# Expert weights of a mixture-of-experts loop loaded from two queues, SyncE's and GpSimd's, in place of one

## The chip, the cores and the metric

The kernel runs on one core of one Trainium2 chip, in float32 throughout. The metric is device time in microseconds (us). A profiled execution also has a span, from its first to its last instruction.

## The reference

One step of a two-layer trunk over 128 context tokens and 128 latent tokens of width 1024. Each layer is an attention block followed by a mixture of 16 experts, of which each token takes two. The experts' part, cut to what matters:

```
def _moe(h, w_router, b_router, w_gate, w_up, w_down):
    ...                                     # gates: two experts of one group for each token
    hid = jax.nn.silu(jnp.einsum('nd,edf->enf', n, w_gate)) * jnp.einsum('nd,edf->enf', n, w_up)
    hid = hid * gates.T[:, :, None].astype(hid.dtype)
    return jnp.einsum('enf,efd->nd', hid, w_down).reshape(b, s, d)
```

`w_gate`, `w_up` and `w_down` are 1024x1024 for each of 16 experts and each of two layers: 96 matrices of 4.2 MB, 403 MB together, each read once from HBM. The outputs are both token groups after two layers and the new keys and values.

## The kernel before

The program is written by hand, engine by engine, with semaphores; the order on each engine is the order in the code, and no scheduler stands between. Each engine's block (`@block.sync`, `@block.gpsimd`, `@block.tensor`) is one instruction stream.

**Pairs and units.** The experts of a layer are worked through in eight pairs, n = 0 to 7. A pair has two experts, e = 0 (the first) and e = 1 (the second), and each matrix is cut into two halves, so that a pair has `MOE_UNITS` = 12 units of 2 MB: k = 0 to 3 are the halves of `w_gate`, 4 to 7 those of `w_up`, 8 to 11 those of `w_down`. Even k belong to e = 0, odd k to e = 1. A unit is written (n, k) below. One load of a unit moves 128 rows of 16 KB, one row to a partition.

**Products.** TensorE works through a pair in six products (`product(n, k, ...)`, L1190), for k = 0, 2, 4, 6, 8, 10. Product (n, k) needs units (n, k) and (n, k+1) together: its 32 matmuls go alternately to the two experts, which occupy the two halves of the array. Between the products stand the scatter of the pair before (L1151, behind product 0) and the transposes and the gather of the next pair (L1246 and L1140, behind product 6).

**The ring.** The units lie in `SLOTS` = 6 buffers of 2 MB (`ring`, with the list `MOE_RING` giving the order). Six is even, so that in the loop three of the slots only ever take first experts' units and three only second experts'. With the last matmul that reads a slot, TensorE raises `moe_used[l]` by one. The load of (n, k) waits until that count is at least `n * MOE_UNITS + (k + 1)`, that is until the unit six places earlier has been used. In pairs 0 to 2 some units go to other buffers (`ahead`, and the tiles named by `kept_rows`): these use none of the ring's turns.

**The loads.** All loads of units are issued by SyncE, in the order of use: pairs 0 to 2 written out (`load_early`, L577), pairs 3 to 6 in a hardware loop over `units_of`, with `load_in_turn` for each unit (wait at L582), and pair 7 by `last_units`: k = 0 to 5 as whole units, and from k = 6 on in pieces of half or a quarter of a unit (`LAST_PIECES`, L640), so that TensorE can begin on a part (`last_product`, L1216). A second round of pairs, in which the counts of tokens would call for it, doesn't take place with these inputs. Behind the experts of layer 0 SyncE goes on to the dense weights of layer 1.

GpSimd computes a few powers (L774), and issues small loads and stores through its own queue. The last thing that it does ahead of a layer's experts is the power for the router's norm.

Of the kernel before, what the change touches and what calls it, by code (L numbers as in the profile page):

```python
# [256 lines left out]
def build(nc, a):  # L257
    ctx = ExitStack()
    with ctx:
# [3 lines left out]
        def sem(name):  # L263
            return ctx.enter_context(nc.semaphore(name))
# [124 lines left out]
        dense_ld = [sem(f"dense_loaded{i}") for i in range(SLOTS)]  # L389
        moe_used = [sem(f"moe_used{l}") for l in range(LAYERS)]  # L390
        moe_ld = [[sem(f"moe_loaded{l}_{i}") for i in range(SLOTS)] for l in range(LAYERS)]
        last_ld = [[sem(f"last_loaded{l}_{i}") for i in range(len(LAST_PIECES))] for l in range(LAYERS)]
        ahead_ld = [[sem(f"ahead_loaded{l}_{e}") for e in range(2)] for l in range(LAYERS)]
        ld_first, ld_const, ld_vec, ld_gb, ld_small, ld_router = (
            sem(n) for n in ("ld_first_const", "ld_const", "ld_vec", "ld_gate_bias", "ld_small", "ld_router"))
# [1 line left out]
        ld_cache = [sem(f"ld_cache{l}") for l in range(LAYERS)]  # L397
        ld_bias = sem("ld_bias")
        turns = sem("turns")
        gbuf_unit_loaded = sem("gbuf_unit_loaded")  # L400
        out_kv = [sem(f"out_kv{l}") for l in range(LAYERS)]
        out_y = sem("out_y")
# [78 lines left out]
        def moe_slot(l, k):  # L481
            return MOE_RING[l][k % SLOTS]
# [76 lines left out]
        def _(sp):  # L559
# [9 lines left out]
            def experts(l):  # L569
# [50 lines left out]

                def units_of(n, i):

                    at = [sp.snap(i * (2 * D * D) + e * D * D) for e in range(2)]
                    for k in range(MOE_UNITS):
                        load_in_turn(k, at[k % 2], n * MOE_UNITS + (k + 1))

                def last_units(n):

                    at = [(2 * (PAIRS - 1) + e) * D * D for e in range(2)]
                    for k in range(LAST_PIECES[0][0]):  # L630
                        load_in_turn(k, at[k % 2], n * MOE_UNITS + (k + 1))
                    for i, (k, c0, c1) in enumerate(LAST_PIECES):
                        w, order = (a["w_up"], "(p h r) -> h p r") if k < 8 else (a["w_down"], "(h p r) -> h p r")
                        for e in range(2):
                            slot = moe_slot(l, k + e - OUTSIDE)
                            src = w[l].rearrange("e k n -> (e k n)")[at[e]:at[e] + D * D].rearrange(order, h=2, p=P)[k // 2 % 2]
                            if c0 == 0:
                                sp.wait_ge(moe_used[l], n * MOE_UNITS + (k + e + 1))
                            cols = slice(D * c0, D * c1)
                            sp.dma_start(flat[slot][:, cols], src[:, cols]).then_inc(last_ld[l][i], 16)  # L640

                def load_first(k):
                    slot = moe_slot(l, k)
# [122 lines left out]
        def _(pool):  # L766
# [33 lines left out]
            def spread_gates(l):  # L800
# [8 lines left out]
                for t in (1, 0):  # L809
                    pool.dma_start(gbuf[:, 2 * t:2 * t + 2, :].rearrange("p u n -> p (u n)"),  # L810
                                   gate_rows[l, t].partition_broadcast(P)).then_inc(gate_spread[t], 16)

            for l in range(LAYERS):
                if l == 1:
                    power("norm", 1, 0, 1)
                    power("norm", 1, 0, 0)
                    pool.wait_ge(filled, fill(("qkv", 1, 0, 1)))
                    rpb = a["c_rpb"]
                    for d in range(3):
                        src = bass.AP(rpb.tensor, rpb.offset + (d + 6) * 31, [[15 * 31, 16], [0, 64], [1, 32]])  # L820
                        pool.dma_start(copies[:, d, :, :], src).then_inc(bias_copied, 16)
                    pool.wait_ge(filled, fill(("qkv", 1, 1, 1)))
                    pool.dma_start(cache[:, 0:1024], a["cache_c_k"][0, 0].rearrange("k h d -> k (h d)")).then_inc(ld_cache[1], 16)
                    pool.dma_start(cache[:, 1024:2048], a["cache_c_v"][0, 0].rearrange("k h d -> k (h d)")).then_inc(ld_cache[1], 16)
                    pool.wait_ge(bias_copied, 48)
                    for r in range(2):
                        for r2 in range(2):
                            src = bass.AP(copies.tensor, copies.offset + (r2 - r + 1) * 64 * 32 + 15, [[31, 64], [3 * 64 * 32, 16], [1, 64]])
                            pool.dma_start(bias[64 * r:64 * r + 64, :, 64 * r2:64 * r2 + 64], src).then_inc(ld_bias, 16)
                power("qk", l, 1)  # L830
                power("qk", l, 0)

                pool.wait_ge(normed, 2 * l + 2)
                pool.wait_ge(*emptied_by(("qkv", l, IN_UNITS[l] - 1, 0)))
                if l == 0:
                    outs = [("new_a_k", 512, 128), ("new_a_v", 640, 128), ("new_b_k", 1280, 512), ("new_b_v", 1792, 512)]
                else:
                    outs = [("new_c_k", 1024, 1024), ("new_c_v", 2048, 1024)]
                for name, at, n in outs:
                    pool.dma_start(a[name], qkv[0][:, at:at + n]).then_inc(out_kv[l], 16)  # L840
                if l == 0:
                    power("sub", 0, 1)
                spread_gates(l)
                if l == 0:
                    power("sub", 0, 0)
                power("norm", l, 1, 1)
                power("norm", l, 1, 0)
            pool.wait_ge(out_kv[0], 64)
            pool.wait_ge(out_kv[1], 32)

# [2 lines left out]
        def _(pe):  # L853
# [272 lines left out]
            def experts(l):  # L1126
# [27 lines left out]
                def product(n, k, banks, lhs, ready, half_done=None):  # L1154
# [6 lines left out]
                    for e in range(2):  # L1161
                        if apart[e]:
                            pe.wait_ge(m["kept_loaded1" if n else f"kept_loaded{e}"], 16 * (KEPT_LOADS[1, l] + KEPT_AGAIN if n else KEPT_LOADS[e, l]))
                        elif slots[e] is None:
                            pe.wait_ge(ahead_ld[l][e], 16 * (n + 1) + (16 if (n, k) == (2, SLOTS + 2) else 0))
                        else:
                            pe.wait_ge(moe_ld[l][slots[e]], (0 if early else 32 * n) + 16 * (1 + turn_of[e] // SLOTS))

                    def weights(e, c, j):
                        if l == 1 and early and (n, k, c) == (0, 0, 3):  # L1170
# [34 lines left out]
                def last_product(n, k, banks, lhs, half_done):  # L1205
# [3 lines left out]
                    for i, (unit, c0, c1) in enumerate(LAST_PIECES):  # L1209
                        if unit != k:  # L1210
                            continue
                        pe.wait_ge(last_ld[l][i], 32)
                        for j in range(2):
                            for c in range(c0, c1):
                                for e in range(2):
                                    ins = pe.matmul(bank[banks[j]][64 * e:64 * e + 64, :], lhs[:, 4 * h + c, 64 * e:64 * e + 64],  # L1216
                                                    rows4[slots[e]][:, c, j * UC:(j + 1) * UC],
                                                    start=(h, c) == (0, 0), stop=(h, c) == (1, 3), tile_position=(0, 64 * e))
                                    if (j, c) == (1, 3):
                                        ins.then_inc(moe_used[l], 1)  # L1220
                            if half_done and (c1, j) == (4, 0):
                                ins.then_inc(half_done, 1)
# [916 lines left out]
```

## Time and profile before

| | |
|---|---|
| time, median of 3 runs | 1244.72 us (1243.37 to 1246.33) |
| the profiled execution: time, span | 1242.9 us, 1241.1 us |
| TensorE busy | 1164.1 us, 94% |
| VectorE, ScalarE, GpSimd busy | 279.8, 187.7, 56.4 us |
| moved by DMA | 494.18 MB, mean 398 GB/s |
| of it from SyncE's queue, from GpSimd's | 485.88 MB, 7.46 MB |
| mean TensorE clock granted | 0.988 of full speed |

All of these but the first row are of one execution under the profiler. Its queue q1 is SyncE's, `hardware_dynamic`; q0 is GpSimd's, `software_dynamic`. A queue's share is the time that its packets took, as a share of the time of the core's 16 DMA engines. "Us to landing" runs from the issue of a DMA to the rise of its semaphore. A matmul group that waited shows in square brackets the idle time ahead of it and what ended it. `PEld` is the load of weights into the array, which runs beside the matmuls.

### The profile page before, as it was taken

The page shows a single profiled execution, that of the slowest core. Times are in us where ns is not written, and L with a number is a line of the kernel's source. Part 1 is how long each engine was busy: PE and PEld are TensorE (multiplying, and loading weights), DVE is VectorE, ACT ScalarE, POOL GpSimd, SP SyncE. Part 2 cuts the span into 40 slices and gives each one's busy share as a digit, 9 for nine tenths or more (in the row PEclk, how much of TensorE's full clock was granted, in tenths as well). Part 3 has the DMA queues.
Part 4 walks back from the last instruction along what each step waited for, and adds up shares of the span by engine and source line. Part 5 has one row for each costly group of instructions (what it writes and reads, how often), then busy time and mean ns, then how long its engine had stood idle before and what let it go on. Part 6 is the DMA issues. An engine that isn't in the chain of part 4 may idle for free.

```text
span 1241.1 us, 13752 instructions
## 1 busy us (share of the span) xinstructions
PE 1164.1 (94%) x5533; PEld 515.1 (42%) x5533; DVE 279.8 (23%) x673; ACT 187.7 (15%) x441; POOL 56.4 (5%) x68
## 2 busy tenths in 40 slices
PE   4999999999988899899999999999999998989898
PEld 1445464443423233334344454753434434343333
DVE  1146533121010101021232354312021110202013
ACT  1224322010000000001021343210001100000010
POOL 0412000000000000000013020000000000000000
PEclk9999999999999999999999999999999999999999
DMA  9999999999999999999997559899999999999997
GB/s 375 383 383 375 414 423 429 424 431 427 429 427 427 429 429 428 429 427 429 420 392 259 203 196 397 339 391 413 426 428 428 428 428 428 428 430 428 427 425 296
DMA packets 60084, 494.18 MB, mean 398 GB/s; under 512 B 5490, under 2 KB 6658, under 8 KB 28420
## 3 DMA queue, kind: packets, MB, share of 16 engines
q1 hardware_dynamic: 56992, 485.88, 94.5%
q0 software_dynamic: 2864, 7.46, 1.9%
q8 instruction: 33, 0.54, 0.2%
q10 hardware_dynamic: 180, 0.17, 0.0%
q14 instruction: 15, 0.12, 0.0%
HBM read 490.72 MB, written 3.16 MB: 398 GB/s over the span
## 4 chain that ended last, share of the span: by engine, by line
PE 72%; DMA 24%; issue 2%; ACT 1%; SPq 1%; DVE 1%; POOL 0%; DVEq 0%
PE bank L1190 39%; PE bank L942 12%; DMA ring<-in_w_up 9%; DMA ring<-in_w_gate 7%; DMA ring<-in_w_down 6%; PE bank L952 3%; PE bank L1140 3%; PE bank L898 3%; PE bank L1151 3%; DMA ring<-in_w_in_ab 2%; PE bank L874 2%; PE bank L1216 1%; PE bank L959 1%; PE bank L997 1%; PE bank L1246 1%
## 5 line engine op out<-in xcount | busy, mean ns | idle before, releaser
L1190 PE MATMUL bank<-ring,hT 128*64 128x512 f32 x2520 | 574.3, 606 | 48.0 <-issue 20.1
L1190 PEld LDWEIGHTS bank<-ring,hT 128*64 128x64 f32 x2520 | 191.2, 139 | 401.6 <-issue 392.8
L942 PE MATMUL bank<-ring,hT 128*128 128x512 f32 x320 | 141.8, 600 | 3.1 <-DMA ring<-in_w_in_ab 2.4
L942 PEld LDWEIGHTS bank<-ring,hT 128*128 128x128 f32 x320 | 60.5, 192 | 79.9 <-issue 77.3
L1983 DVE TENSOR_TENSOR work<-work,bank 128x512 f32<-128x512 f32 x56 | 38.5, 688 | 164.0 <-PE bank L1151 163.8
L1976 DVE TENSOR_TENSOR work<-work,bank 128x512 f32<-128x512 f32 x32 | 22.0, 688 | 223.6 <-PE bank L1190 198.8
L1190 PE MATMUL bank<-work,hT 128*64 128x512 f32 x284 | 69.5, 593 | 0.0
L1140 PE MATMUL bank<-work 128*128 128x128 f32 x512 | 60.3, 275 | 0.0
L1140 PEld LDWEIGHTS bank<-work 128*128 128x128 f32 x512 | 58.7, 192 | 1.6 <-issue 1.6
L1519 ACT ACTIVATE hT<-bank 128x512 f32<-128x512 f32 x32 | 19.0, 595 | 256.9 <-PE bank L1246 256.9
L2024 DVE COPY work<-bank 128x512 f32<-128x512 f32 x14 | 9.7, 692 | 207.3 <-PE bank L1190 207.3
L1151 PE MATMUL bank<-work 128*128 128x512 f32 x112 | 51.8, 605 | 0.0
L898 PE MATMUL bank<-ring,cond 128*32 128x512 f32 x384 | 47.4, 616 | 2.4 <-DMA ring<-in_w_mod 2.0
L1216 PE MATMUL bank<-ring,hT 128*64 128x512 f32 x192 | 42.9, 595 | 4.0 <-DMA ring<-in_w_down 4.0
L1964 DVE TENSOR_TENSOR work<-work,bank 128x512 f32<-128x512 f32 x32 | 22.0, 688 | 106.9 <-ACT work L1528 106.9
L952 PE MATMUL bank<-ring,work 128*128 128x512 f32 x96 | 42.5, 595 | 0.3 <-DVE work L1793 0.3
L1190 PEld LDWEIGHTS bank<-work,hT 128*64 128x64 f32 x284 | 22.8, 137 | 41.8 <-issue 41.4
L1546 ACT ACTIVATE work<-bank 128x512 f32<-128x512 f32 x14 | 8.4, 597 | 191.2 <-PE bank L1190 191.2
L1528 ACT ACTIVATE work<-bank 128x512 f32<-128x512 f32 x32 | 19.1, 597 | 108.5 <-PE bank L1190 108.5
L1151 PEld LDWEIGHTS bank<-work 128*128 128x128 f32 x112 | 20.1, 189 | 31.5 <-issue 31.5
L1454 ACT ACTIVATE work<-bank,nm 128x256 f32<-128x256 f32 (+1 forms) x64 | 26.0, 421 | 29.7 <-DVE nm L1766 29.7
L774 POOL TENSOR_TENSOR ss<-ss,const 128x1 f32<-128x1 f32 x8 | 4.4, 556 | 553.1 <-DVE ss L1640 498.6
(220 smaller groups left out, 754.4 us busy)
## 6 DMA issues: line engine op xcount, KB each, us to landing
ring<-in_w_gate SPq DMA_DIRECT2D x56, 2048.0 KB, 17.7
ring<-in_w_up SPq DMA_DIRECT2D x50, 2048.0 KB, 17.2
ring<-in_w_down SPq DMA_DIRECT2D x46, 2048.0 KB, 17.0
ring<-in_w_mod SPq DMA_DIRECT2D x23, 2048.0 KB, 11.1
work<-in_w_up SPq DMA_DIRECT2D x8, 2048.0 KB, 15.2
ring<-in_w_down SPq DMA_DIRECT2D x14, 1024.0 KB, 14.7
ring<-in_w_in_c SPq DMA_DIRECT2D x6, 2048.0 KB, 21.1
ring<-in_w_in_ab SPq DMA_DIRECT2D x4, 2048.0 KB, 21.6
```

The costliest lines, as they stand in the source:

```text
L874: ins = pe.transpose(b[:, i * P:(i + 1) * P], src, K("ident"))
L898: ins = pe.matmul(out, cond[:, 2 * k + r, :], cols, start=(k, r) == (0, 0), stop=(k, r) == (3, 1), tile_position=(0, 32 * j))
L942: ins = pe.matmul(b[:, 0:n], hT[:, c, t * P:(t + 1) * P], w[:, c, 0:n], start=i == 0, stop=i == DC - 1)
L952: ins = pe.matmul(b[:, :], oT(l, t, c), w[:, c, :], start=c == 0, stop=c == DC - 1)
L1140: ins = pe.matmul(to[:, c * P:(c + 1) * P], htok(t)[:, at:at + P], pick[:, t, :], start=t == 0, stop=t == 1)
L1151: pe.matmul(bank[4 + 2 * t + h][:, :], GT[:, t, :], yd[:, h * UC:(h + 1) * UC], start=True, stop=True).then_inc(m["scattered"], 1)
L1190: ins = pe.matmul(bank[banks[j]][64 * e:64 * e + 64, :], lhs[:, 4 * h + c, 64 * e:64 * e + 64], weights(e, c, j), start=(h, c) == (0, 0), ...
L1216: ins = pe.matmul(bank[banks[j]][64 * e:64 * e + 64, :], lhs[:, 4 * h + c, 64 * e:64 * e + 64], rows4[slots[e]][:, c, j * UC:(j + 1) * UC] ...
L1454: ins = act.activation(PR[:, j % 2, h, 0:nk], bank_of(("S", l, t, b, e))[:, i * nk:(i + 1) * nk], ACT.Exp, bias=nm[:, j % 2, h:h + 1], sca ...
L1964: dve.tensor_tensor(hid[:, half], sg[:, half], bank[h][:, :], ALU.mult).then_inc(m["gate_taken"], 1)
L1976: dve.tensor_tensor(hid[:, half], hid[:, half], bank[2 + h][:, :], ALU.mult).then_inc(m["hid_done"], 1)
L1983: dve.tensor_tensor(y[:, t, cols], y[:, t, cols], bank[4 + 2 * t + h][:, :], ALU.add).then_inc(m["y_added"], 1)
```

## The change

For pairs 3 to 7 of each layer the loads of the second expert's whole units (odd k: six a pair in pairs 3 to 6, and k = 1, 3, 5 of pair 7) are issued by GpSimd, each after its own wait on `moe_used[l]` with the number it had on SyncE. SyncE keeps the even ones, with their waits, and both experts' pieces from k = 6 of pair 7 on. GpSimd's loads raise semaphores of their own (`pool_ld`, three a layer), and TensorE waits for these in place of the ring's (`moe_ld`) where e = 1. The semaphores of the last pieces are shared by the two layers. Sizes, sources, destinations, slots and the order within each expert are as they were.

```diff
+        pool_ld = [[sem(f"pool_loaded{l}_{i}") for i in range(SLOTS // 2)] for l in range(LAYERS)]
...
                 def units_of(n, i):
 
-                    at = [sp.snap(i * (2 * D * D) + e * D * D) for e in range(2)]
-                    for k in range(MOE_UNITS):
-                        load_in_turn(k, at[k % 2], n * MOE_UNITS + (k + 1))
+                    at = sp.snap(i * (2 * D * D))
+                    for k in range(0, MOE_UNITS, 2):
+                        load_in_turn(k, at, n * MOE_UNITS + (k + 1))
...
-                    for k in range(LAST_PIECES[0][0]):
-                        load_in_turn(k, at[k % 2], n * MOE_UNITS + (k + 1))
+                    for k in range(0, LAST_PIECES[0][0], 2):
+                        load_in_turn(k, at[0], n * MOE_UNITS + (k + 1))
...
+            def experts(l):
...
+                def load_in_turn(k, at, wait):
+                    w, half = matrix_of(k)
+                    slot = moe_slot(l, k - OUTSIDE)
+                    pool.wait_ge(moe_used[l], wait)
+                    pool.sem_inc(turns, 1)
+                    flat_w = w[l].rearrange("e k n -> (e k n)")[bass.ds(at, D * D)]
+                    order = "(h p r) -> h p r" if k >= 8 else "(p h r) -> h p r"
+                    pool.dma_start(flat[slot], flat_w.rearrange(order, h=2, p=P)[half]).then_inc(pool_ld[l][k % SLOTS // 2], 16)
+
+                def units_of(n, i):
+
+                    at = pool.snap(i * (2 * D * D) + D * D)
+                    for k in range(1, MOE_UNITS, 2):
+                        load_in_turn(k, at, n * MOE_UNITS + (k + 1))
...
+                    for k in range(1, LAST_PIECES[0][0], 2):
+                        load_in_turn(k, at, n * MOE_UNITS + (k + 1))
+
+                with pool.Fori(3, PAIRS - 1) as i:
+                    units_of(i, i)
...
+                last_units(more * PAIRS + (PAIRS - 1))
...
                 power("norm", l, 1, 1)
                 power("norm", l, 1, 0)
+                experts(l)
...
-                        else:
+                        elif early or not e:
                             pe.wait_ge(moe_ld[l][slots[e]], (0 if early else 32 * n) + 16 * (1 + turn_of[e] // SLOTS))
+                        else:
+                            pe.wait_ge(pool_ld[l][(k + 1) % SLOTS // 2], 32 * n + (16 * (1 + turn_of[e] // SLOTS) - (80 if (k + 1) % SLOTS == 5 else 64)))
...
-                        pe.wait_ge(last_ld[l][i], 32)
+                        pe.wait_ge(last_ld[i], 32 * (l + 1))
```

SyncE, the body of the loop over pairs 3 to 6 in layer 0, before; the numbers behind `ring` are the slots, the two experts' units alternate, and the register instruction between two loads sets the next wait.

```order
L577 DMA ring4<-in_w_gate 128x4096
L581 REGISTER_ALU
L577 ISA
L577 DMA ring5<-in_w_gate 128x4096
L581 REGISTER_ALU
L577 ISA
L577 DMA ring3<-in_w_gate 128x4096
L581 REGISTER_ALU
L577 ISA
L577 DMA ring1<-in_w_gate 128x4096
L581 REGISTER_ALU
L577 DMA ring2<-in_w_up 128x4096
```

And in the changed kernel, the same body from its first load to its last:

```order
L578 DMA ring4<-in_w_gate 128x4096
L582 REGISTER_ALU
L578 ISA
L578 DMA ring3<-in_w_gate 128x4096
L582 REGISTER_ALU
L578 DMA ring2<-in_w_up 128x4096
L582 REGISTER_ALU
L578 DMA ring4<-in_w_up 128x4096
L582 REGISTER_ALU
L578 DMA ring3<-in_w_down 128x4096
L582 REGISTER_ALU
L578 ISA
```

The loads to slots 5, 1 and 0 have left SyncE's stream, which now holds six loads a pair, to slots 4, 3 and 2.

GpSimd, from the last power ahead of the experts of layer 0, in the changed kernel (before, the next instruction behind this power was layer 1's first):

```order
L775 TENSOR_TENSOR ss<-ss,const 128x1 x2
L840 UNCONDITIONAL_BRANCH
L840 ISA
L826 ISA
L826 DMA ring5<-in_w_gate 128x4096
L822 REGISTER_ALU
L826 ISA
L826 DMA ring1<-in_w_gate 128x4096
L822 REGISTER_ALU
L826 DMA ring0<-in_w_up 128x4096
L822 REGISTER_ALU
L826 DMA ring5<-in_w_up 128x4096
```

The first of these loads is unit (3, 1). It stands behind no load of pairs 0 to 2, all of which SyncE still issues.

## Rows read from the trace of the kernel before

**Rows 1.** The page: DMA engines, busy tenths and GB/s in 40 slices of 31 us.

```profile
...
DMA  9999999999999999999997559899999999999997
GB/s 375 383 383 375 414 423 429 424 431 427 429 427 427 429 429 428 429 427 429 420 392 259 203 196 397 339 391 413 426 428 428 428 428 428 428 430 428 427 425 296
...
```

**Rows 2.** Busy time by stretch: columns in the first row, DMA share and GB/s last.

```profile
...
core 0: us, PE busy (x) PEld busy (x) DVE busy (x) ACT busy (x) POOL busy (x), PEclk, DMA share, GB/s
...
253.00:303.00 50.00, 50.00 (x244) 19.84 (x242) 7.74 (x17) 4.46 (x8) 0.00 (x0) 1.00 1.01 428
...
400.00:450.00 50.00, 43.72 (x206) 17.84 (x202) 7.04 (x16) 4.45 (x8) 0.00 (x0) 0.97 1.01 428
...
```

**Rows 3.** TensorE, 328 to 354 us.

```profile
...
328.71 7.09 PE L1190 MATMUL bank<-work,hT 128*64 128x512 f32 x32
336.04 7.09 PE L1190 MATMUL bank<-ring,hT 128*64 128x512 f32 x32 [0.24 <-issue]
345.97 7.09 PE L1190 MATMUL bank<-ring,hT 128*64 128x512 f32 x32 [2.84 <-DMA ring<-in_w_gate]
...
```

**Rows 4.** L577, issues between 320 and 326 us, time to landing.

```profile
...
L577 SPq DMA_DIRECT2D ring<-in_w_gate x2: 332/332/333, 324.3 to 324.9; - x2
...
DMA to landing us min/median/max: 26.3/28.5/30.6
```

**Rows 5.** DMA queues, 400 to 450 us.

```profile
...
DMA packets 1472, 21.41 MB, mean 428 GB/s; under 512 B 165, under 2 KB 165, under 8 KB 165
...
q1 hardware_dynamic: 1472, 21.41, 100.6%
...
```

**Rows 6.** GpSimd behind the experts of layer 0.

```profile
...
636.20 0.55 POOL L774 TENSOR_TENSOR ss<-ss,const 128x1 f32<-128x1 f32 x1 [454.13 <-DVE ss L1640]
...
655.17 0.55 POOL L824 DMA_DIRECT2D work<-in_cache_c_v  x1
...
```

**Rows 7.** TensorE, 600 to 633 us, the tail of layer 0.

```profile
...
600.56 7.09 PE L1190 MATMUL bank<-ring,hT 128*64 128x512 f32 x32 [0.50 <-DMA ring<-in_w_up]
...
614.44 1.61 PE L1246 MATMUL bank<-const,work 128*128 128x128 f32 x8
...
625.31 7.09 PE L1216 MATMUL bank<-ring,hT 128*64 128x512 f32 x32 [1.42 <-DMA ring<-in_w_down]
632.39 1.98 PE L1237 MATMUL bank<-work 128*128 128x512 f32 x4
...
```

**Rows 8.** SyncE's queue, 299 to 344 us.

```profile
...
317.43 7.85 SPq L577 DMA_DIRECT2D ring<-in_w_gate  x4
343.24 10.85 SPq L577 DMA_DIRECT2D ring<-in_w_up  x4
...
```

**Rows 9.** Every DMA issue of the kernel: a small store, us to landing.

```profile
...
out_y_sample<-x SPq DMA_DIRECT2D x2, 256.0 KB, 2.1
...
```

**Rows 10.** DMA queues, 134 to 137 us.

```profile
...
q1 hardware_dynamic: 107, 0.87, 68.5%
q0 software_dynamic: 104, 0.42, 34.2%
...
```

**Rows 11.** DMA queues, 758 to 761 us.

```profile
...
q0 software_dynamic: 236, 0.85, 70.3%
q1 hardware_dynamic: 24, 0.38, 29.3%
...
```

**Rows 12.** DMA queues, 156 to 165 us.

```profile
...
DMA packets 367, 3.83 MB, mean 426 GB/s; under 512 B 35, under 2 KB 35, under 8 KB 163
...
q1 hardware_dynamic: 366, 3.82, 100.7%
...
```

**Rows 13.** DMA queues, 656 to 660 us.

```profile
...
q0 software_dynamic: 96, 0.39, 25.1%
...
```

**Rows 14.** DMA queues, 745 to 753 us.

```profile
...
DMA packets 684, 3.49 MB, mean 436 GB/s; under 512 B 135, under 2 KB 135, under 8 KB 540
...
```

**Rows 15.** DMA queues, 130.6 to 140 us.

```profile
...
DMA packets 1005, 3.90 MB, mean 415 GB/s; under 512 B 32, under 2 KB 32, under 8 KB 768
...
```

## What the change was predicted to do

> **What bounds the kernel now.** I began with the page's slices. The DMA engines stand at 9 tenths from the start to some 640 us and again from some 800 us to the end, at 424 to 431 GB/s wherever experts are loaded at full rate; only around layer 1's attention do they fall, to 5 [rows 1]. The busy times by stretch show what this means for TensorE: between 253 and 303 us it is busy for the whole 50 us, between 400 and 450 us for 43.72, while the engines show a share of 1.01 and 428 GB/s in both [rows 2]. So TensorE is the faster of the two: a pair is 12 loads of 2.097 MB, which take 58.8 us at 428 GB/s, 4.9 us each. In the first pairs it lives on units loaded ahead; from layer 0's pair 2 on it waits, as for the gate units of product (3, 0) at 345.97 us [rows 3]. SyncE's own time doesn't enter: the loads that it issued at 324.3 and 324.9 us landed only after 26.3 and 30.6 us [rows 4]. The end of the experts is set by bytes over rate.
>
> The queue list gives the form of the load. From 400 to 450 us there were 1472 packets, 165 of them under 512 B; the other 1307 carry 21.41 MB, 16 KB each: one row of a unit. They cost 1.006 x 50 / 21.41 = 2.35 us of all engines per MB [rows 5].
>
> **What moves.** GpSimd takes 24 loads a layer in pairs 3 to 6 and 3 in pair 7: 54 loads, 113 MB. While both queues feed the engines SyncE moves as much; 226 MB at 428 GB/s is a stretch of 529 us. Here a change of rate counts: 1% is 5.3 us.
>
> **Issue.** One costs SyncE 0.33 us [rows 4]. For GpSimd the nearest row is a cache's load, 0.55 us [rows 6]; it needs six in 58.8 us and has nothing else to do for 454 us ahead of the power at 636.20 us [rows 6]. What hides the issue is the backlog of two loads or more, 9.8 us. On GpSimd only its own next loads stand behind a waiting one, and behind layer 0's that power, over 30 us after product (7, 4) began at 600.56 us [rows 7]. Without the cover 27 issues a layer cost 0.22 us more each, 12 us in all. I take 0.
>
> **Which load goes first.** SyncE issued (3, 0) at 317.43 us and the next three up to 325.3 us [rows 8]. Before, (3, 1) and (3, 3) stood behind everything older. Now they are in a queue of their own and take part at once. Before, (3, 3) landed at 324.9 + 30.6 = 355.5 us [rows 4]; stepping back by 4.9 us a load, (2, 11) landed at about 335.9 us, and TensorE began product (2, 10) at 336.04 [rows 3]. GpSimd's two loads can overtake by 9.8 us at most, since (3, 5) has to wait for a slot. So (2, 11) lands at 345.7 us, product (2, 10) ends at 352.8, and only then are (3, 4) and (3, 5) issued, (3, 4) at 343.24 before [rows 8]. Do the engines run dry? What was issued by 324.9 us lasts until 355.5 us as before, 2.7 us longer. A load's start costs less: a store of 256 KB, 0.6 us of transfer, landed after 2.1 us [rows 9]. Product (3, 0) starts some 7 us late but finds (3, 1) to (3, 3) landed or nearly so, and the lag is made up in a few products, each of which takes TensorE 7.1 us and the engines 9.8. Cost 0. If the margin failed, each us beyond it would cost a us a layer.
>
> **Tail.** With half for each queue, both units of a product land when the second of them landed before. From 600.56 us TensorE has four products of 7.1 us and transposes of 1.61 us, up to 630.5 us, where its last product ended at 632.39 [rows 7]. So (7, 5) may land 1.9 us late for nothing. Where GpSimd gets more than half, the last bytes are SyncE's, and nothing is lost either. The sharing itself is seen twice: from 134 to 137 us 104 packets of GpSimd's (4 KB) ran beside 107 of SyncE's (8 KB) [rows 10]; from 758 to 761 us GpSimd's 4 KB packets moved 0.85 MB beside 0.38 MB of SyncE's 16 KB packets [rows 11]. GpSimd's queue wasn't held back in either. I take half and half, and 0.
>
> The Trainium skill ("DMA: Bandwidth & Descriptors", section "Queues, rings and completion order") says that each engine takes turns between queues packet by packet. The first stretch agrees, 104 to 107; the second doesn't, since by that rule GpSimd's small packets would have had a fifth of the bytes. By the rule the sum would be the same here as long as both sides use 16 KB packets.
>
> **A GpSimd packet's price.** No row shows one of 16 KB. SyncE's 4 KB packets: from 156 to 165 us there were 128 (163 less the 35 small ones), 0.52 MB; of 9.06 us in all the other 3.30 MB take 7.75, which leaves 2.52 us per MB [rows 12]. GpSimd's, loading a cache: 0.251 x 4 / 0.39 = 2.57 us per MB [rows 13]. The 0.05 is 0.003 us a packet on one engine. Taken per packet, 8 packets an engine a load and 54 loads give 432 x 0.0033 = 1.4 us; taken per byte, 5.7 us. I take 1.4, since the size changes and the count of events is what a packet's overhead goes with. Below, a gain isn't excluded: see the third rival.
>
> **Sum.** The profiled execution took 1242.9 us (span 1241.1), and 1.4 makes 1244.3. The median of the runs is 1.8 above that execution, so 1246.1 us: no change that could be told, for I count 0.2% (2.5 us) as what a measurement here can tell.
>
> **The rivals.**
>
> *SyncE's queue is favoured* (slower). If it gets clearly more than half, the pieces of (7, 6) and (7, 7), 9.8 us of transfer, go ahead of (7, 5), and the tail starts that much late: 9.8 - 1.9 = 7.9 us a layer, 15.8 in both, 1262 us. It decides from 1.9 us of lag. The two stretches of rows 10 and 11 speak against it. 0.13.
>
> *GpSimd's rows are cut into 4 KB packets* (slower): 2.57 in place of 2.35 us per MB on 113 MB is 25 us, 1271 us, and by turns of packets the first rival comes on top. For it speaks only that every large GpSimd packet in the trace is of 4 KB, and so are the rows there. 0.10. The Trainium skill ("DMA: Bandwidth & Descriptors", section "SWDGE vs HWDGE vs iDMA") prefers packets of at most 4096 B where GpSimd builds them; no run here shows such a cut, since every row was short enough.
>
> *Two queues fill the engines better* (faster). A packet of one queue can hide the other's gap. From 745 to 753 us, with both at work, 436 GB/s were moved [rows 14], 1.9% above 428: 9.9 us over the stretch, 1235 us at best; a third to a half of it, some 1241, is likelier, because GpSimd's part there was stores. 0.22.
>
> *A few engines are slowed by GpSimd's queue* (slower). A load is complete with its slowest engine, and all of them are full, so the mean rate falls. With GpSimd's packets in the mix 415 GB/s were moved from 130.6 to 140 us [rows 15]; against 428 that is 3%, 16 us over 529, but SyncE's rows of 8 KB and less explain part of it, so 5 to 16 us, 1251 to 1262. 0.09. The Trainium skill ("DMA: Bandwidth & Descriptors", section "Latency and other measured facts") puts a like slowness of two engines down to the rings that GpSimd writes, as a guess; this profile shows no single engine.
>
> **How the numbers follow.** The forecast has 0.46, its own range being 1243 to 1248. Faster is 0.22; slower is 0.13 + 0.10 + 0.09 and 0.02 of the forecast's upper end, 0.34; the same 0.44. The range runs from 1239, which leaves out the better part of the third rival's gain, 0.08, to 1263, which leaves out the cut rows, 0.10.
>
> **What will show it.** Right: SyncE and GpSimd each some 50% of the engines between 400 and 450 us, 1307 large packets there, and 428 GB/s; product (2, 10) about 10 us late, product (3, 6) on its old time; the last products of both layers as before. Wrong: more packets than 1472 in that window (cut rows); a rate other than 427 to 429; idle engines near 355 us; or (7, 5) landing after 602.5 us while SyncE's pieces are in.

## The result, and the profile after

The changed kernel took 1246.64 us (median of 20 runs, 1244.24 to 6849.65), the kernel before beside it 1243.77 us (20 runs, 1242.37 to 1246.76). The ratio is 1.0025, 95% interval 1.0015 to 1.0036: some 3 us slower, a little past the 0.2% that had been set as the limit of what can be told. The forecast was 1246.1 us and "no change". One of the 20 runs took 6849.65 us; the next longest took 1259.0. It is left out of the ratio, no later run of any kernel repeated it, and it stays unexplained. The profiled execution took 1245.49 us, span 1243.8, that is 2.6 and 2.7 more than before.

**The page**, whose slices answer to [rows 1], differs in one place worth a look:

```profile
...
GB/s 374 391 375 375 414 423 429 423 432 428 427 382 428 429 429 428 427 429 428 422 394 281 204 186 398 337 384 419 423 429 424 427 429 428 429 428 427 429 423 300
...
```

Slice 12 (342 to 373 us, counting from 1) has 382 GB/s in place of 427. The other slices of layer 0's pairs have 422 to 432, before 420 to 431. This is the part in which the second queue takes up its work in layer 0.

**In the steady part** of layer 0 the queues look as predicted (compare [rows 2, 5]):

```profile
...
DMA packets 1469, 21.45 MB, mean 429 GB/s; under 512 B 160, under 2 KB 160, under 8 KB 160
...
q0 software_dynamic: 735, 10.73, 50.5%
q1 hardware_dynamic: 734, 10.72, 50.3%
...
```

735 packets for 10.73 MB beside 734 for 10.72: half and half, and GpSimd's rows go as one packet of 16 KB each, not cut. Their price is 0.505 x 50 / 10.73 = 2.353 us of all engines per MB, SyncE's 2.346. On 113 MB that makes 0.8 us by this row; the prediction had 1.4.

**Busy times by stretch** (last columns: granted clock, DMA share, GB/s):

```profile
...
core 0: us, PE busy (x) PEld busy (x) DVE busy (x) ACT busy (x) POOL busy (x), PEclk, DMA share, GB/s
335.00:345.00 10.00, 1.00 (x6) 0.11 (x2) 0.00 (x0) 0.00 (x0) 0.00 (x0) 0.67 1.00 424
345.00:355.00 10.00, 9.04 (x36) 3.25 (x38) 0.69 (x1) 0.54 (x1) 0.00 (x0) 0.81 0.78 331
355.00:365.00 10.00, 10.00 (x40) 3.72 (x36) 2.12 (x4) 0.06 (x1) 1.06 (x2) 1.00 0.98 390
400.00:450.00 50.00, 43.01 (x198) 17.07 (x194) 7.73 (x17) 3.37 (x6) 2.64 (x5) 0.97 1.01 429
1060.00:1110.00 50.00, 44.46 (x208) 18.65 (x205) 7.73 (x17) 4.14 (x8) 2.64 (x5) 0.97 1.01 428
...
```

429 and 428 GB/s in the steady parts of the two layers, as before. But from 345 to 355 us the engines moved 331 GB/s at a share of 0.78, and then 390; before it was 426 and 428. This is (428 - 331) x 10 + (428 - 390) x 10 us, 1.35 MB, or 3.2 us of all engines. A closer look at the hole:

```profile
...
345.00:348.00 3.00, 2.04 (x6) 0.85 (x8) 0.00 (x0) 0.00 (x0) 0.00 (x0) 0.50 1.03 437
351.00:352.00 1.00, 1.00 (x6) 0.31 (x4) 0.69 (x1) 0.00 (x0) 0.00 (x0) 1.00 0.81 344
352.00:353.00 1.00, 1.00 (x8) 0.37 (x6) 0.00 (x0) 0.00 (x0) 0.00 (x0) 1.00 0.65 279
353.00:354.00 1.00, 1.00 (x8) 0.40 (x6) 0.00 (x0) 0.00 (x0) 0.00 (x0) 1.00 0.12 49
354.00:354.50 0.50, 0.50 (x4) 0.15 (x2) 0.00 (x0) 0.04 (x1) 0.00 (x0) 1.00 0.00 0
354.50:355.00 0.50, 0.50 (x4) 0.15 (x2) 0.00 (x0) 0.50 (x1) 0.00 (x0) 1.00 0.08 33
355.00:355.50 0.50, 0.50 (x4) 0.15 (x2) 0.00 (x0) 0.06 (x1) 0.41 (x1) 1.00 0.13 33
355.50:356.00 0.50, 0.50 (x6) 0.21 (x4) 0.00 (x0) 0.00 (x0) 0.12 (x1) 1.00 2.26 492
357.00:358.00 1.00, 1.00 (x6) 0.31 (x4) 0.00 (x0) 0.00 (x0) 0.00 (x0) 1.00 0.84 360
...
```

The rate fell from 351 us on, to 49 GB/s between 353 and 354. From 354.0 to 355.0 us a single packet started, the 16 KB that make the 33 GB/s of the last half microsecond, and the flow came back at 355.5. A window counts a packet where it starts, so the shares of such short windows are rough; the old rate stands again from 358 on. By the bytes missing from 352 to 358 us the hole is 3.2 us of all engines.

The 16 engines did not run out together. A load raises its semaphore sixteen times, in the trace's single records, and a product waits for the last of these; each load's raises have the same spacing as those of the load before it, shifted by 4.9 us, as if each belonged to one engine. For (3, 2), the last load queued, fifteen came between 352.2 and 354.2 us and the last at 355.63, mean 353.4. The last packet ended at 355.15 us, 0.5 before the last raise. So one engine was some 1.5 us behind the others and worked almost until the flow came back, while the average engine was done at about 352.9 us (the mean raise less that 0.5, an estimate). Before, the raises of (3, 3) lie alike: fifteen from 352.1 to 353.9 us, the last at 355.5. The spread is not the second queue's work.

**Why they ran empty** is read from the views below. First SyncE's queue (start, length, issues in the group):

```profile
...
317.63 7.20 SPq L578 DMA_DIRECT2D ring<-in_w_gate  x2
354.53 7.20 SPq L578 DMA_DIRECT2D ring<-in_w_up  x2
...
```

And GpSimd's issues, each with the wait ahead of it:

```profile
...
318.20 0.59 POOL L826 DMA_DIRECT2D ring<-in_w_gate  x1 [135.94 <-PE bank L1232]
325.40 0.54 POOL L826 DMA_DIRECT2D ring<-in_w_gate  x1 [6.61 <-issue]
355.10 0.53 POOL L826 DMA_DIRECT2D ring<-in_w_up  x1 [29.16 <-PE bank L1232]
...
```

GpSimd issued (3, 1) at 318.20 us and (3, 3) at 325.40, each with 0.53 to 0.59 us (0.55 predicted). They landed 15.4 and 18.0 us later, at 333.6 and 343.4, while the same trace has SyncE's (3, 0) and (3, 2), issued at 317.6 and 324.5, landing after 33.1 and 31.1 us. In between both queues moved bytes at once (320 to 328 us):

```profile
...
q1 hardware_dynamic: 130, 1.88, 55.3%
q0 software_dynamic: 92, 1.51, 44.6%
...
```

So the older loads in SyncE's queue had to give way. The landing of the two units (2, 10) and (2, 11):

```profile
...
L578 SPq DMA_DIRECT2D ring<-in_w_down x2: 327/379/431, 310.5 to 310.9; - x2
...
DMA to landing us min/median/max: 28.0/31.5/35.0
```

310.9 + 35.0 = 345.9 us, where the prediction had 345.7 and before it was about 335.9. TensorE (compare [rows 3]):

```profile
...
328.91 7.09 PE L1232 MATMUL bank<-work,hT 128*64 128x512 f32 x32
345.96 15.31 PE L1232 MATMUL bank<-ring,hT 128*64 128x512 f32 x64 [9.96 <-issue]
...
365.05 20.94 PE L1232 MATMUL bank<-ring,hT 128*64 128x512 f32 x96
...
408.34 7.09 PE L1232 MATMUL bank<-ring,hT 128*64 128x512 f32 x32 [2.73 <-DMA ring<-in_w_gate]
...
```

After product (2, 8) TensorE stood for 9.96 us, and products (2, 10) and (3, 0) together took 15.31 us in place of two times 7.09 less the overlap, 13.95. The first window of the fine view shows why: from 345 to 348 us the granted clock was 0.50, the lower of TensorE's two levels, 1.2 GHz. It cost this pair 1.4 us. The Trainium skill ("TensorE: Matmul & The Clock Gate", section "What's actually happening") has the clock fall when the engine is idle; the row agrees. Only at 354.53 us did SyncE issue (3, 4), at 355.10 GpSimd (3, 5). The last load queued until then, (3, 2), landed at 324.5 + 31.1 = 355.6 us. The lag stays: product (3, 6), the third in the row at 365.05 us, began at 379.0 (375.19 before), product (4, 0) at 408.34 (404.69 before), and the layer's last product (compare [rows 7]) ended 2.7 us late:

```profile
...
589.89 20.88 PE L1232 MATMUL bank<-ring,hT 128*64 128x512 f32 x96
610.58 7.07 PE L1258 MATMUL bank<-ring,hT 128*64 128x512 f32 x32
...
627.97 7.09 PE L1258 MATMUL bank<-ring,hT 128*64 128x512 f32 x32 [1.39 <-DMA ring<-in_w_down]
635.06 1.98 PE L1279 MATMUL bank<-work 128*128 128x512 f32 x4
...
```

The row at 589.89 holds the three products up to (7, 4), 96 matmuls without a wait. The waits of the pieces behind it are 0.16 and 1.39 us, before 0.60 and 1.42.

**Accounting by layer**, from the profiles. For layer 0 I take the instant at which TensorE's small group behind the last scatter begins: 634.21 us before, 636.88 after, +2.67. For layer 1 I take the time from its first expert product to its last scatter: 433.95 before, 434.02 after. So in this pair of executions all of the 2.7 us came in layer 0, where the bytes went missing between 345 and 365 us, and the 0.8 us of the packets doesn't show.

### The profile page after: what moved, and what is told of

Same layout as the page of the kernel before. It is cut to its first block, busy times and chain, and to the rows that moved or that the text cites. A ratio compares the mean times of both kernels' runs of the same rounds, so it can differ in the third digit from the quotient of the medians.

```text
span 1243.8 us, 13780 instructions
## 1 busy us (share of the span) xinstructions
PE 1163.7 (94%) x5533; PEld 514.6 (41%) x5533; DVE 279.6 (22%) x673; ACT 187.6 (15%) x441; POOL 85.0 (7%) x122
## 4 chain that ended last, share of the span: by engine, by line
PE 65%; DMA 31%; issue 2%; ACT 1%; DVE 1%; SPq 0%; POOLq 0%; POOL 0%; DVEq 0%
PE bank L1232 34%; DMA ring<-in_w_gate 13%; PE bank L982 12%; DMA ring<-in_w_up 11%; DMA ring<-in_w_down 5%; PE bank L992 3%; PE bank L938 3%; PE bank L1180 2%; DMA ring<-in_w_in_ab 2%; PE bank L1191 2%; PE bank L914 2%; PE bank L1258 1%; PE bank L999 1%; PE bank L1037 1%; PE bank L1271 1%
## 5 line engine op out<-in xcount | busy, mean ns | idle before, releaser
L826 POOL DMA_DIRECT2D ring<-in_w_gate x20 | 10.7, 534 | 445.0 <-PE bank L1232 426.8
L775 POOL TENSOR_TENSOR hss<-hss,const 128x28 f32<-128x28 f32 (+2 forms) x6 | 22.6, 3764 | 116.2 <-DVE hss L1641 116.2
```

Of the source, the lines that this page charges most:

```text
L775: pool.tensor_tensor(v, v, K("mhalf")[:, 0:v.shape[1]], ALU.pow).then_inc(power_taken, 1)
```

## The experiments

The expectations speak of two theories. **A**: the loss is the overtaking at the place where the second queue begins. **B**: it is a cost of the second queue itself, spread over its 54 loads. Ratios are against the kernel before, run on the same chip, with 95% intervals; "layer 0" is the shift of the instant defined above, in one profiled execution. Kernels 1 and 5 have the same program for layer 0 and stand at 0.0 and +1.7, so a difference of that size between two rows can be chance.

| kernel | median us | ratio | layer 0 |
|---|---|---|---|
| the change | 1246.64 | 1.0025 [1.0015, 1.0036] | +2.7 |
| 1: first two on SyncE, layer 0 | 1244.96 | 1.0018 [1.0003, 1.0034] | 0.0 |
| 2: before, only the first two on GpSimd | 1246.78 | 1.0025 [1.0016, 1.0034] | +2.5 |
| 3: before, the first four on GpSimd | 1251.32 | 1.0059 [1.0047, 1.0072] | +12.1 |
| 10: before, only the first on GpSimd | 1243.03 | 0.9998 [0.9989, 1.0006] | -0.1 |
| 5: first two on SyncE, both layers | 1243.62 | 1.0004 [0.9993, 1.0015] | +1.7 |
| 4: 34 idle matmuls behind (2, 8) | 1246.44 | 1.0023 [1.0011, 1.0034] | +5.5 |
| 6: 16 and 16 idle matmuls | 1246.01 | 1.0021 [1.0011, 1.0030] | +3.2 |
| 9: 16 and 26 idle matmuls | 1246.78 | 1.0033 [1.0019, 1.0047] | +1.5 |
| 7: GpSimd's rows in 4 KB pieces | 1263.45 | 1.0157 [1.0139, 1.0175] | +15.2 |
| 8: SyncE's rows in 4 KB pieces | 1262.34 | 1.0150 [1.0132, 1.0169] | +12.4 |

### 1. Without the overtaking in layer 0

```diff
+                if l == 0:
+                    for k in (0, 1, 2, 3, 4, 6, 8, 10):
+                        slot = moe_slot(l, k - OUTSIDE)
+                        sp.wait_ge(moe_used[l], 3 * MOE_UNITS + (k + 1))
+                        load(k, (6 + k % 2) * D * D, flat[slot], first_ld[k // 2] if k % 2 else moe_ld[l][slot])
-                with sp.Fori(3, PAIRS - 1) as i:
+                with sp.Fori(4 if l == 0 else 3, PAIRS - 1) as i:
...
```

SyncE keeps (3, 1) and (3, 3) of layer 0, and GpSimd begins there with (3, 5).

> The changed kernel, except that in layer 0 units (3, 1) and (3, 3) stay in SyncE's queue; GpSimd begins with (3, 5), so nothing overtakes pair 2's loads. Two loads of 256 B into a scratch row take the place of the two on GpSimd's semaphores. Theory A (the loss is one pause of the DMA engines near 355 us, made by the two loads that overtake): the span falls back by 2.7 us to about 1241.1, ratio to the kernel before 1.000, product (2, 10) of layer 0 begins near 336.0 us again, and 428 GB/s are moved from 345 to 400 us. Theory B (each GpSimd packet costs more than SyncE's, over all 54 loads): 52 of the 54 loads are still GpSimd's, so the ratio stays at 1.0025.

Layer 0 behaved as A says. Two stretches, the one in which the engines were short in the changed kernel, and one of layer 1:

```profile
...
345.00:355.00 10.00, 8.99 (x33) 2.99 (x34) 0.00 (x0) 0.00 (x0) 0.00 (x0) 0.83 1.01 428
...
950.00:955.00 5.00, 5.00 (x26) 1.89 (x24) 0.17 (x1) 0.60 (x1) 0.53 (x1) 1.00 1.00 390
...
```

428 GB/s from 345 to 355 us, and the layer is back at its old end. The ratio isn't 1: 1.0018, its interval just free of 1. In this execution layer 1 took 435.88 us, 1.9 more than before, with 390 GB/s from 950 to 955 us, which makes 0.4 us of it; the rest isn't placed. The kernel still overtakes in layer 1, where I had expected nothing.

### 2, 3 and 10. The overtaking alone, with two loads, four and one

Based on the kernel before; `first_ld` holds k = 1 and 3, then 0 to 3, then 1 alone. All else stays with SyncE. Pair 3's loads are written out for this, and the semaphores of the last pieces are shared as in the change; kernel 10 has the same edits, so it also shows what they cost: nothing.

```diff
+                if l == 0:
+                    for k in first_ld:
+                        pool.wait_ge(moe_used[l], 3 * MOE_UNITS + (k + 1))
+                        src = a["w_gate"][l].rearrange("e k n -> (e k n)")[(6 + k % 2) * D * D:(7 + k % 2) * D * D]
+                        pool.dma_start(flat[moe_slot(l, k - OUTSIDE)], src.rearrange("(p h r) -> h p r", h=2, p=P)[k // 2]).then_inc(first_ld[k], 16)
...
```

> The complement: the kernel before, except that units (3, 1) and (3, 3) of layer 0 are GpSimd's, and nothing else. Theory A: the whole loss with 2 of the 54 loads, ratio 1.0025, product (2, 10) near 346 us, the engines paused near 355 us. Theory B: 2/54 of the loss, 0.1 us, ratio 1.000.

> As the run with the first two, but all four gate units of pair 3 of layer 0, (3, 0) to (3, 3), are GpSimd's: the overtaking doubled. Theory A: at half and half the four take 19.6 us of transfer and SyncE's backlog at 318 us is 17.8 us, so (2, 11) lands near 353.6 us, product (2, 10) ends near 362.4 at the slow clock, and the engines stand still from about 355.5 us (last byte 2 us earlier) until some 364: 8 to 11 us are lost, ratio 1.0065 to 1.009. Theory B: 4/54 of the loss, ratio 1.000.

> The kernel before, except that unit (3, 1) of layer 0 alone is GpSimd's: the overtaking halved against the run with two. Theory A: 4.9 us are overtaken, (2, 11) lands near 340.8 us, product (2, 10) ends near 348 to 349.5, 6 us before what is queued runs out, so the engines never stop and nothing is lost: ratio 1.000. A loss in proportion to the overtaking would give half of that with two loads, 1.0012.

Two loads on GpSimd, with 52 fewer than in the change, lose all that the change loses. TensorE in kernel 2:

```profile
...
345.62 15.42 PE L1203 MATMUL bank<-ring,hT 128*64 128x512 f32 x64 [9.44 <-issue]
...
```

And SyncE's queue there:

```profile
...
354.24 7.67 SPq L578 DMA_DIRECT2D ring<-in_w_up  x4
...
```

The same wait, the same slow pair of products, the same late issue. B is refuted as the cause of this loss. With four loads product (2, 10) came at 353.49 us (worked out ahead as 353.6) and the next issue on SyncE at 363.54; the engines stood for nearly a whole stretch. TensorE in kernel 3:

```profile
...
353.49 16.83 PE L1203 MATMUL bank<-ring,hT 128*64 128x512 f32 x64 [10.05 <-issue]
...
```

And the busy times by stretch:

```profile
...
355.00:365.00 10.00, 10.00 (x39) 3.33 (x37) 0.69 (x1) 0.60 (x1) 0.00 (x0) 0.78 0.12 28
...
```

The loss was 7.3 us by the ratio and 8.0 by the medians, in the profiled execution 12, which is the longest of the six: the expectation of 8 to 11 was a little high for the median. With one load product (2, 10) came at 340.94 us (340.8 worked out), the issue at 350.71, and nothing was lost. TensorE in kernel 10:

```profile
...
340.94 16.56 PE L1203 MATMUL bank<-ring,hT 128*64 128x512 f32 x64 [4.53 <-issue]
...
```

And SyncE's queue:

```profile
...
350.71 7.67 SPq L578 DMA_DIRECT2D ring<-in_w_up  x4
...
```

One, two and four loads that overtake delay product (2, 10) by 4.9, 9.6 and 17.5 us, yet they cost 0, about 3 and 7 to 12 us. That is the form of a margin used up, not of a price per load. Kernel 10 also shows that the slow clock does no harm while the margin holds. It covered more of product (2, 10) than in the change (busy times by stretch, kernel 10):

```profile
...
340.00:343.00 3.00, 2.06 (x6) 0.86 (x8) 0.00 (x0) 0.00 (x0) 0.00 (x0) 0.50 1.01 431
343.00:346.00 3.00, 3.00 (x8) 0.80 (x6) 0.00 (x0) 0.00 (x0) 0.00 (x0) 0.50 1.00 426
352.00:355.00 3.00, 3.00 (x16) 1.09 (x14) 0.00 (x0) 0.00 (x0) 0.00 (x0) 1.00 0.97 393
...
```

0.50 up to 346 us, product (2, 10) took 9.8 us (350.71 - 340.94), 1.2 more than in the change, and the engines still had work: the bytes queued were the same, and the issue came 3.8 us sooner.

### 5. No overtaking of the first products in either layer

Kernel 1's edit for both layers.

> The changed kernel, except that in both layers units (3, 1) and (3, 3) stay in SyncE's queue, so that no GpSimd load overtakes pair 2's; GpSimd begins with (3, 5). Two loads of 256 B a layer into a scratch tensor take the place of those on GpSimd's semaphores. Theory A2 (overtaking costs 2.5 to 2.7 us in layer 0, and 0 to 2 us in layer 1, where the run with only layer 0 cured lost 1.9): the ratio is 1.000, inside 0.999 to 1.001. Theory B (the queue's packets cost more): 50 of 54 loads are GpSimd's, 1.0018 or more as in that run.

1.0004 [0.9993, 1.0015]: the loss is gone from the times, and nothing is gained over before. In the profiled execution some of it had moved. GpSimd's first loads are now (3, 5) and (3, 7), and (3, 2) and (3, 3) give way to them. TensorE in kernel 5:

```profile
...
346.17 7.09 PE L1244 MATMUL bank<-ring,hT 128*64 128x512 f32 x32 [2.94 <-DMA ring<-in_w_gate]
...
363.06 23.63 PE L1244 MATMUL bank<-ring,hT 128*64 128x512 f32 x96 [5.96 <-issue]
...
```

And a stretch of its busy times:

```profile
...
370.00:380.00 10.00, 10.00 (x48) 3.55 (x46) 1.38 (x2) 0.76 (x2) 0.53 (x1) 1.00 0.87 338
...
```

Product (3, 2) waited 5.96 us, and from 370 to 380 us the engines were at 0.87. Kernel 1, with the same layer 0, had a wait of 3.04 us at this product and 431 GB/s in that stretch, so this stop comes in some executions only. Wherever the second queue begins, something gives way; here less depends on it.

### 4, 6 and 9. TensorE kept busy through its wait

```diff
+                            if l == 0 and early and (n, k) == (2, 10):
+                                keep_busy((16, 26)[e], bank[2])
```

`keep_busy` adds matmuls of 128x128 with no use (each shows as two in the trace), ahead of the waits for units (2, 10) and (2, 11). Kernel 9 is shown; kernel 6 has 16 and 16, kernel 4 one batch of 34 behind product (2, 8). This asks how much of the loss is the slow clock after the wait.

> The changed kernel with 34 idle matmuls of 128 columns (into a bank that nothing reads) between products (2, 8) and (2, 10) of layer 0, some 9.2 us, while TensorE waits for (2, 11). After its idle 10 us in the changed kernel TensorE took 15.3 us for products (2, 10) and (3, 0), 1.3 us more than two products at full clock. Theory A with the slow clock as a part: product (2, 10) takes 7.1 us in place of 8.2 to 8.8, (3, 4) and (3, 5) are issued 1.2 to 1.7 us sooner, and as much of the 2.7 us comes back: span near 1242.3, ratio about 1.0013. If the clock has no part, the ratio stays at 1.0025.

> The changed kernel with 16 idle matmuls of 128 columns ahead of TensorE's wait for (2, 10) and 16 more ahead of that for (2, 11) in layer 0, each batch some 4 us, so that the batches end before the units land and delay nothing. If the slow clock is a part of the loss, product (2, 10) takes 7.1 us and 1.2 to 1.7 us of the 2.7 come back, ratio 1.0010 to 1.0015. If it is not, the ratio stays at 1.0025 and the time lost is all made by the 9.8 us of overtaking and the start of a load.

> As the run kept busy by halves, whose batches ended 2.65 us before (2, 11) landed and left products (2, 10) and (3, 0) at 15.65 us, but with 26 matmuls in the second batch, to end some 0.3 us before it lands. If a short idle time keeps the clock up, the two products take 14.1 us, (3, 4) is issued near 353 us in place of 354.5, 1.2 to 1.5 us of the loss come back, ratio 1.0012 to 1.0015. If (2, 11) lands early in some executions, the batch delays product (2, 10) by up to 1 us there. If the clock has no part: ratio 1.0025, and the products at full clock without a gain.

Kernel 4 tells nothing: in its profiled execution the batch ran past the landing, and product (2, 10) began at 350.18 us. In kernel 6 the batches ended 2.65 us before the landing (TensorE, kernel 6):

```profile
...
335.88 7.41 PE L962 MATMUL bank<-const 128*128 128x128 f32 x64
345.94 15.65 PE L1234 MATMUL bank<-ring,hT 128*64 128x512 f32 x64 [2.65 <-DMA ring<-in_w_down]
...
```

and the pair still took 15.65 us: the granted clock was 1.00 from 346.0 to 346.6 us and 0.50 from 347 to 350, so it fell after the product had begun. In kernel 9 they reached to it (TensorE):

```profile
...
346.18 13.95 PE L1234 MATMUL bank<-ring,hT 128*64 128x512 f32 x64
...
```

And SyncE's queue in kernel 9:

```profile
...
353.41 7.20 SPq L578 DMA_DIRECT2D ring<-in_w_up  x2
...
```

13.95 us, (3, 4) issued at 353.41 in place of 354.53, and layer 0 lost 1.5 us in place of 2.7. So in the trace the issue came 1.1 us sooner and the layer ended 1.2 sooner. Kernels 1 and 5 differ by more than that with one and the same layer 0, and the times don't bear it out either: 1.0033 [1.0019, 1.0047], where 1.0012 to 1.0015 was expected. In that execution layer 1 lost 2.8 us, by a stretch of its own (busy times, kernel 9):

```profile
...
955.00:960.00 5.00, 5.00 (x26) 2.00 (x24) 0.00 (x0) 0.60 (x1) 0.53 (x1) 1.00 0.69 246
...
```

Whether the clock's part would show in the times is left open; the executions of layer 1 (below) vary by more.

### 7 and 8. Small packets on one of the queues

Kernel 7 cuts each of GpSimd's loads into four of 4 KB per row; kernel 8 does it with SyncE's whole units of pairs 3 to 7.

```diff
+                    for c in range(4):
+                        cols = slice(D * c, D * (c + 1))
+                        pool.dma_start(flat[slot][:, cols], flat_w.rearrange(order, h=2, p=P)[half][:, cols]).then_inc(pool_ld[l][k % SLOTS // 2], 16)
...
```

> The changed kernel with each of GpSimd's 54 units loaded by four DMAs of 4 KB rows: 216 issues of 0.55 us, four times the packets. If the engines take turns by packets, GpSimd gets a fifth of the bytes while both queues are full: then SyncE's units land first, each product waits for GpSimd's, (7, 5) lands behind the pieces of (7, 6) and (7, 7), and the tail costs 8 to 13 us a layer; with 2.52 to 2.57 us per MB on 113 MB (19 to 25 us) the ratio is 1.025 to 1.04. If the sharing is by bytes, the tail costs nothing: 1.015 to 1.02. If 4 KB rows cost no more beside 16 KB ones, 1.0025 and the tail's part.

> The mirror image: GpSimd's units whole, SyncE's whole units of pairs 3 to 7 by four DMAs of 4 KB rows. The same price per MB on the same bytes, but now GpSimd is favoured, so the tail and the steady state wait for SyncE's units, which costs nothing by the prediction's reading. Expected by turns of packets: 1.012 to 1.02, below the run with GpSimd's rows cut by the tail's 16 to 26 us. If the sharing is by bytes, the two runs agree.

This is the prediction's rival of cut rows, made to happen. Queues of kernel 7 from 322 to 340 us, with a backlog in both:

```profile
...
q1 hardware_dynamic: 421, 6.11, 80.1%
q0 software_dynamic: 418, 1.56, 21.5%
...
```

And from 500 to 550 us:

```profile
...
q1 hardware_dynamic: 803, 11.60, 54.8%
q0 software_dynamic: 2542, 9.28, 46.2%
...
```

2.49 us per MB for GpSimd's 4 KB, 2.36 for SyncE's 16 KB, and 418 GB/s together, 2.4% under 428: 12.7 us over the 529, and stops of the kind above on top. The measured loss is 19.5 us by the ratio; the rival's price had been 25. Kernel 8, with the small packets on the other side, loses the same within 1 us. It has 418 and 420 GB/s between 450 and 550 us, but 401 from 400 to 450 and 406 from 1060 to 1110; what holds it back there isn't explained. Rows of 4 KB cost this, on either queue. In the first view the turns go by packets when both queues have a backlog: 418 small ones moved 1.56 MB, a fifth of the bytes, beside 421 with 6.11 MB. The Trainium skill ("DMA: Bandwidth & Descriptors", section "Queues, rings and completion order") says so, and this row agrees. Even so no tail grew out of it: product (7, 4) of kernel 7 began at 604.45 us without a wait, and the 16 to 26 us by which kernel 8 was to be faster didn't come. My reading, not tried by itself: what rules the sharing over a pair is that each queue can only load what has become free.

## Why the prediction was right in most steps and wrong in one

**Right.** The kernel is bound by bytes over rate, before and after. The queues share by half, at the old rate of 428 to 429 GB/s. GpSimd's packet costs nearly what SyncE's costs (0.8 us in all, 1.4 taken). Issue and tail cost nothing. The instants of the start were right to tenths: 345.9 us for the landing of (2, 11), 355.6 for the last load queued.

**Luck.** The time of 1246.1 us lies 0.5 from the measured median because two errors met: the loss came to 2.9 us in place of 1.4, and the median before, of 20 runs, was 0.95 lower than that of the three that I had started from.

**Wrong: "Which load goes first", with its "Do the engines run dry? What was issued by 324.9 us lasts until 355.5 us as before, 2.7 us longer. A load's start costs less", and the "Cost 0".** Experiments 2 and 5 put the loss there by their times and experiment 1 by its trace, and 10 and 3 show the margin from both sides. Three things ate it, by the trace:

- The products. (3, 4) was to be issued at 352.8 us and came at 354.53. TensorE had stood for 10 us and ran the next products slower. In kernel 9, where that was prevented, the issue came at 353.41: this is 1.1 us of the 1.7, in one trace, and the times don't show it.
- The backlog's end. 355.6 us is when the slowest of the 16 engines had done its part. The average engine had run out at about 352.9, 2.7 us earlier, so for it the margin of 2.7 us never existed. The prediction took the landing of a load for the end of all engines' work; the raises of (3, 3) before, 352.1 to 355.5 us, had the spread already. This part is read from the traces, not tried by itself.
- The start. From the issue at 354.53 us to the return of the flow at 355.5 it took 1.0 us, and the first packet of each engine took 0.9 to 1.8 us in place of 0.61, some 0.6 more in the mean. I had priced it at no more than the 2.1 us of a small store [rows 9], which was enough; but I had set it against a margin that wasn't there.

Put right, the sum for the average engine is 354.5 + 1.0 - 352.9 = 2.6 us and the 0.6 of the first packets, 3.2 us, which is what the missing bytes give; the layer lost 2.7.

"The lag is made up in a few products" was wrong too, and follows from it. TensorE makes its own lag up, but engine time that was empty can't be: product (4, 0) came 3.65 us late and the layer ended 2.67 us late. The sign named in the prediction, idle engines near 355 us, is what the trace shows.

**Layer 1** I hadn't worked out at all; I said only that a failed margin costs in each layer. Its time from first product to last scatter was, with overtaking in it, 434.02 (the change), 435.88, 435.16, 434.55 and 436.73 us (kernels 1, 4, 6, 9), mean 435.3; without it 433.95 (before), 433.04, 433.54, 434.24 and 434.60 (kernels 2, 3, 10, 5), mean 433.9. So 0 to 2.8 us, 1.4 in the mean, over five single executions each, against a scatter of 1.7 us in layer 0 between kernels 1 and 5. Kernel 1 against kernel 5 (1.0018 and 1.0004) points the same way, but their intervals overlap. That kernel 2, which does not overtake in layer 1, lost as much as the change is not explained by this sum (2.5 against 2.7 + 1.4); the intervals, 1.9 to 4.5 us for the change and 2.0 to 4.2 for kernel 2, leave room for it. It stays open.

**The rivals.** Better filled engines: refuted, 429 and 428 GB/s. (Its 1235 us had been reckoned without the packets' 1.4.) Cut rows: refuted by 735 packets for 10.73 MB; its price, when made to happen, is 19 us against the kernel before. SyncE favoured: refuted, halves and a tail without a new wait; with a backlog in both queues, from 322 to 340 us, GpSimd had 262 packets and SyncE 254. The prediction read [rows 11] as speaking against turns by packets. They don't: SyncE's two loads had been issued only at 757.5 and 757.9 us, and from 758 to 759 us its queue moved one packet beside 89, so its loads had hardly begun. Slowed engines: refuted by the same rate and by the same spread of the raises before and after; the 415 GB/s of [rows 15] came with rows of 4 and 8 KB, and kernels 7 and 8 show the like from 4 KB rows alone (418 and 420 at best). The slower side came about by the step that I had priced at zero, not by a rival.

## What to carry to other kernels

A stream of loads that waits for its bytes gains nothing from a second queue when the first already fills the engines (428 GB/s here with one and with two). When an ordered stream is split, ask what the second queue's first loads overtake: every one delays what is needed next by about its own transfer, the delay passes on to the release of room, and if that comes later than the bytes still queued last, the engines stand. Compare the two with the product slowed after its wait, with the end of the average engine and not the landing, which is that of the slowest, and with the start of a load. Here the first two of these took 1.7 and 2.7 us off a margin reckoned at 2.7.

## What the runs showed of the hardware that was not expected

- GpSimd's queue moved 16 KB rows as single packets at SyncE's price, 2.353 against 2.346 us per MB, and 1469 packets in 50 us in place of 1472.
- Rows of 4 KB on one of the two queues made the kernel 1.5% slower than before, whichever queue had them, at 418 to 420 GB/s in its better stretches in place of 428.
- With a backlog in both queues the engines took turns one packet to one, whatever the size: 262 beside 254 of mostly 16 KB each in the change, 418 of GpSimd's 4 KB beside 421 of SyncE's 16 KB in kernel 7.
- The 16 raises of one load came apart, one engine behind the others, and a landing is the last of them: they lay over 3.4 us (352.2 to 355.6), before the change as after, and the last came 0.5 us behind the last packet's end. With the engines empty a new load's bytes flowed 1.0 us behind its issue; GpSimd's first load, issued at 318.20 us among SyncE's, had moved one packet by 322.
- TensorE's clock stood at 0.50 for the start of the product behind a wait of 4.5 or 10 us. The wait of 2.65 us behind small matmuls in kernel 6 brought the slow pair too (15.65 us), but a wait of 2.84 us before, behind products, did not [rows 3]. It isn't the small matmuls: before, product (3, 6) took 8.78 us behind a wait of 2.55 us, with a clock of 0.56 from 375.5 to 378 us, and product (3, 0) took 8.78 us in kernel 1 behind 2.95 us and 7.09 in kernel 5 behind 2.94. What sets the cases apart wasn't tried.
- One run of 6849.65 us among 20 of the changed kernel, never seen again.
